# A decoder layer on one core: the order of TensorE's tiled fp32 steps, and of ScalarE's and VectorE's steps with them

## What is computed

```
h = x
z = rms_norm(h, norm_mix) @ w_in                          # 1024 x 3328
y_rwkv = rwkv7_time_mix(z[:, :1792], ...)                 # 8 heads x 64, a recurrence over tokens
y_moba = moba_attention(q, k, v from z[:, 1792:])         # 8 heads x 64, causal, one block of 256
h = h + concat(y_rwkv, y_moba) @ w_mix_out                # 1024 x 1024
h = h + cross_attention(rms_norm(h), rms_norm(mem))       # 4 heads x 256; w_xq, w_xkv, w_xo
a = square(relu(rms_norm(h, norm_ffn) @ w_ff1))           # 1024 x 4096
h = h + a @ w_ff2                                         # 4096 x 1024
out = rms_norm(h, norm_final)
```

## Time and profile before

| what | value |
|---|---|
| median of 3 runs | 471.38 us (470.81 to 471.77) |
| profiled execution, its own time | 470.57 us |
| its span, first to last instruction | 468.8 us |
| mean granted TensorE clock | 0.996 |
| PE busy | 453.8 us, 97% |
| DVE, ACT, POOL busy | 322.0, 236.6, 35.1 us |

### The profile page before, as it was taken

How to read it: one execution, slowest core, us unless ns; L and a number is a source line. 1 busy time by engine, 2 the same in 40 slices (tenths; PEclk the granted TensorE clock), 3 DMA queues, 4 the chain that set the end, 5 groups by cost and what they waited for, 6 DMA issues and landing times.

```text
span 468.8 us, 10481 instructions
## 1 busy us (share of the span) xinstructions
PE 453.8 (97%) x4470; PEld 410.1 (87%) x4470; DVE 322.0 (69%) x487; ACT 236.6 (50%) x373; POOL 35.1 (7%) x51
## 2 busy tenths in 40 slices
PE   4999999989999999999999999999999999999994
PEld 4999999989899879999998898888888888888883
DVE  4688999897485557668766368876555656574746
ACT  5789833252444426436444455545465545454534
POOL 8200000000000000071000001340000000000000
PEclk9999999999999999999999999999999999999998
DMA  7973534606050432462552165655546565756502
GB/s 246 334 226 119 180 95 142 215 5 184 3 194 15 153 119 89 137 225 89 180 181 89 35 189 189 218 181 179 180 147 213 185 197 166 251 185 218 188 2 89
DMA packets 60385, 73.05 MB, mean 156 GB/s; under 512 B 1314, under 2 KB 49524, under 8 KB 60340
## 3 DMA queue, kind: packets, MB, share of 16 engines
q1 hardware_dynamic: 60260, 72.14, 48.3%
q0 software_dynamic: 80, 0.26, 0.1%
HBM read 71.35 MB, written 1.05 MB: 154 GB/s over the span
## 4 chain that ended last, share of the span: by engine, by line
PE 90%; DVE 4%; DMA 1%; SPq 1%; ACT 1%; issue 1%; ACTq 0%; DVEq 0%
PE bank L534 13%; PE bank L549 11%; PE bank L550 10%; PE bank L551 10%; PE bank L566 6%; PE bank L568 6%; PE bank L567 6%; PE bank L536 6%; PE bank L915 2%; DMA raw<-in_w_in 1%; PE bank L502 1%; PE bank L503 1%; PE bank L504 1%; PE bank L939 1%; PE bank L488 1%
## 5 line engine op out<-in xcount | busy, mean ns | idle before, releaser
L1622 DVE TENSOR_TENSOR w_lo<-raw,w_hi 128x1024 fp32r<-128x1024 f32 x130 | 160.2, 1239 | 67.2 <-ACT w_hi L1114 67.1
L1114 ACT ACTIVATE w_hi<-raw 128x1024 fp32r<-128x1024 f32 x130 | 136.8, 1057 | 111.0 <-PE bank L551 51.8
L534 PE MATMUL bank<-op,w_hi 128*128 128x512 f32 x256 | 89.1, 398 | 0.0
L549 PE MATMUL bank<-op,w_hi 128*128 128x256 f32 x288 | 83.7, 291 | 0.2 <-DVE w_lo L1622 0.2
L550 PE MATMUL bank<-op,w_hi 128*128 128x256 f32 x288 | 81.4, 283 | 0.0
L551 PE MATMUL bank<-op,w_lo 128*128 128x256 f32 x288 | 81.4, 283 | 0.0
L536 PE MATMUL bank<-op,w_lo 128*128 128x256 f32 x224 | 62.8, 281 | 0.0
L549 PEld LDWEIGHTS bank<-op,w_hi 128*128 128x128 f32 x288 | 55.1, 191 | 1.3 <-issue 0.9
L550 PEld LDWEIGHTS bank<-op,w_hi 128*128 128x128 f32 x288 | 55.2, 192 | 0.2
L551 PEld LDWEIGHTS bank<-op,w_lo 128*128 128x128 f32 x288 | 55.1, 191 | 0.0
L534 PEld LDWEIGHTS bank<-op,w_hi 128*128 128x128 f32 x256 | 46.4, 188 | 8.9
(11 more groups left out here) (275 smaller groups left out, 712.6 us busy)
## 6 DMA issues: line engine op xcount, KB each, us to landing
raw<-in_w_ff SPq DMA_DIRECT2D x32, 1024.0 KB, 5.4
raw<-in_w_in SPq DMA_DIRECT2D x12, 1024.0 KB, 5.5
raw<-in_w_xkv SPq DMA_DIRECT2D x8, 1024.0 KB, 5.3
raw<-in_w_mix_out SPq DMA_DIRECT2D x4, 1024.0 KB, 5.0
raw<-in_w_xq SPq DMA_DIRECT2D x4, 1024.0 KB, 5.0
raw<-in_w_xo SPq DMA_DIRECT2D x4, 1024.0 KB, 5.7
xval<-in_x SPq DMA_DIRECT2D x2, 512.0 KB, 4.7
raw<-in_w_in SPq DMA_DIRECT2D x2, 512.0 KB, 5.7
```

Source lines behind the costliest of these rows:

```text
L534: last = mm(b[:, :], wh[:, k, :], op_both[0][:, :, k, :], start=first, stop=final)
L549: mm(dst, wh[:, k, :], op_hi[which][:, k, :], start=first, stop=False)
L1114: op(view(w_hi), r, ACT.Copy).then_inc(hi_done, 1)
L1622: tt(view(w_lo), r, view(w_hi).bitcast(f32), ALU.subtract).then_inc(lo_done, 1)
```

## The change

The lists of calls of PE, ACT and DVE are written in another order. No instruction is added or removed, no shape changes, and one wait is added, on DVE in `bonus`. On PE the tiled steps stand together more often: `mats` in one piece for three, `outq` in one for four, `psi` in one for two, `pair_scores` and `pair_values` beside other tiled steps. The number of unbroken stretches of fp32 steps between quarters goes from 49 to 40; those with a tiled step in them from 26 to 14. A change of the tile from one instruction to the next occurs 64 times before and 43 times after; of these, 29 and 17 go from the whole array to a tile, as many go back, and 6 and 9 go from one tile to another. 23 and 10 stretches end in a tiled step, 26 and 30 in one of the whole array. The core of the diff:

```diff
 # PE
+            load(0, 0)
             params(0)
-            load(0, 0)
...
-            dense(2)
+            dense(1)
             params(1)
-            dense(2)
+            dense(5)
             spread(0)
...
-            dense(2)
-            vtokens()
             bonus()
             dense(2)
+            vtokens()
+            dense(1)
             mats(0, 0)
             mats(0, 1)
-            dense(1)
             mats(0, 2)
             mats(0, 3)
-            dense(3)
             mats(1, 0)
...
+            dense(4)
             right(0)
             right(1)
-            load(1, 2)
-            dense(4)
-            load(1, 3)
+            dense(1)
             right(2)
-            right(3)
-            dense(1)
             join(0, 0)
             join(0, 1)
-            dense(2)
+            right(3)
             join(1, 0)
-            dense(3)
+            join(1, 1)
+            dense(4)
             pair_scores(0)
-            join(1, 1)
-            dense(1)
             solve(0)
...
+            pair_values(0)
             outq(0, 0)
-            pair_flip(0)
             outq(0, 1)
             outq(0, 2)
-            pair_values(0)
-            dense(1)
-            pair_scores(1)
-            dense(1)
             outq(0, 3)
...
+            outq(1, 3)
+            pair_scores(1)
+            dense(6)
+            phi(0)
+            phi(1)
+            pair_flip(1)
...
             turn(3)
-            dense(1)
             values(3)
-            dense(46)
+            dense(58)
             rms(3)
-            dense(9)
+            dense(29)
             residual(0)
+            dense(6)
             residual(1)
-            dense(34)
+            dense(12)
             residual(2)
+            dense(32)
             residual(3)
-            dense(53)
+            dense(6)
 # ACT
             hi(1)
-            stats(0)
             hi(2)
             hi(3)
+            stats(0)
             hi(4)
+            stats(1)
             hi(5)
             follow(0)
-            stats(1)
...
 # DVE
             def bonus():
                 dve.wait_ge(pe_bonus, 1)
+                dve.wait_ge(dve_shift, 7)
...
             square(1)
-            lo(72)
+            add(2, 1)
+            lo(73)
+            lo(74)
             hidden(1)
...
```

More of the change, by code:

```diff
@@ L1031, in _ @@
             dense(1)
-            pair_flip(2)
             state(1)
-            dense(1)
+            pair_scores(2)
             state(2)
-            pair_values(2)
             dense(1)
             state(3)
+            dense(4)
+            state(4)
+            pair_flip(2)
             dense(1)
-            state(4)
-            dense(1)
+            pair_values(2)
             state(5)
@@ L1391, in _ @@
             right(0)
+            load(1, 2)
             hi(24)
-            load(1, 2)
+            hi(25)
             right(1)
+            right(2)
+            join()
             load(1, 3)
-            right(2)
             right(3)
-            join()
-            hi(25)
             hi(26)
@@ L1406, in _ @@
             pair_flip(0)
+            hi(29)
             pair_values(0)
-            hi(29)
             hi(30)
+            outq(0)
+            hi(31)
             pair_scores(1)
-            hi(31)
-            pair_flip(1)
-            outq(0)
             outq(1)
@@ L1416, in _ @@
             hi(33)
+            pair_flip(1)
             pair_values(1)
-            pair_scores(2)
             hi(34)
@@ L1514, in _ @@
             part(4, 1)
+            follow(36)
             hi(82)
-            follow(37)
             part(5, 0)
             hi(83)
+            hi(84)
+            follow(37)
+            hi(85)
             part(5, 1)
-            hi(84)
+            hi(86)
             follow(38)
-            hi(85)
-            hi(86)
             hi(87)
+            part(6, 0)
             hi(88)
-            part(6, 0)
-            rms(3)
-            residual(0)
             hi(89)
@@ L1601, in _ @@
             hi(129)
+            residual(3)
             finish()
@@ L2051, in _ @@
             load(0, 3)
+            params(1)
             lo(1)
-            diagonal_of(0)
-            params(1)
             lo(2)
             lo(3)
+            copies(0)
+            diagonal_of(0)
             spread_copy(0)
+            take(0)
             lo(4)
-            take(0)
+            copies(1)
+            lo(5)
             follow(0)
-            lo(5)
+            lo(6)
             take(1)
-            lo(6)
-            copies(1)
-            lo(7)
             follow(1)
             take(2)
+            lo(7)
             lo(8)
+            sides()
             lo(9)
+            follow(2)
             diagonal_of(1)
-            follow(2)
             take(3)
             sums()
+            lo(10)
+            key_norm()
             follow(3)
+            key_root()
             spread_copy(1)
-            key_norm()
-            lo(10)
-            key_root()
             lo(11)
+            keys(0)
             take(4)
-            keys(0)
             keys(1)
@@ L2101, in _ @@
             lo(18)
-            sides()
+            follow(6)
+            lo(19)
             load(1, 0)
+            take(8)
+            load(1, 1)
             bonus()
-            lo(19)
             lo(20)
-            load(1, 1)
-            take(8)
-            bonus_bias()
             mats(0)
-            take(9)
+            mats(1)
             lo(21)
             lo(22)
+            take(9)
             lo(23)
-            mats(1)
             blocks()
@@ L2146, in _ @@
             phi(2)
-            pair_values(1)
-            pair_scores(2)
-            pair_weigh(2)
-            take(15)
             lo(33)
             lo(34)
+            take(15)
+            pair_values(1)
             state(1)
             state(2)
+            pair_scores(2)
+            bonus_bias()
+            state(3)
             take(16)
-            state(3)
+            pair_weigh(2)
             lo(35)
+            state(4)
             lo(36)
-            state(4)
             state(5)
+            pair_values(2)
+            lo(37)
             state(6)
-            lo(37)
+            pair_scores(3)
             states_out()
-            pair_values(2)
+            pair_weigh(3)
             lo(38)
-            pair_scores(3)
+            deviation()
             take(17)
-            pair_weigh(3)
-            deviation()
             lo(39)
-            take(18)
             normalize()
             lo(40)
+            take(18)
             lo(41)
@@ L2193, in _ @@
             operand("mix", 0)
+            operand("mix", 1)
             lo(50)
-            operand("mix", 1)
             operand("mix", 2)
+            lo(51)
             operand("mix", 3)
+            lo(52)
+            rms(2)
             take(24)
-            lo(51)
-            lo(52)
+            take(25)
             lo(53)
-            rms(2)
-            take(25)
+            scores(0)
             lo(54)
-            scores(0)
             weigh(0)
+            lo(55)
             take(26)
-            lo(55)
             lo(56)
+            scores(1)
+            weigh(1)
+            take(27)
+            values(0)
             lo(57)
-            scores(1)
-            take(27)
-            weigh(1)
+            scores(2)
             lo(58)
-            values(0)
-            scores(2)
+            lo(59)
             weigh(2)
-            lo(59)
             values(1)
```

297 lines of the change are left out of this document (144 added, 153 removed).

## The result

The change makes the kernel slower: 486.39 us as the median of 4 runs (485.89 to 487.57) against 471.40 (470.81 to 471.77), a ratio of 1.0323 with a 95% interval of 1.0311 to 1.0335. The prediction was 467.6. The profiled execution took 485.89 us with a span of 483.9, 15.1 us more than the one before.

The account below looks back on a forecast made before the run. PE's own instruction list was taken as the bound, plus its few waits. Borders and tails -3.34, waits -0.9 and -0.2, start +0.65 gave -3.8 us, from 471.38 to 467.6, range 465.5 to 469.8.

Parts of the forecast that it names:

- The sum over borders: On PE, fewer ways into and out of tiled stretches and fewer stretch ends would save 3.34 us.
- The prices: Cost of a tiled stretch on PE beyond its work: 0.09 us going in, 0.11 coming back, plus the tail.
- the tail: Time at the end of a tiled stretch that is no work: 0.14 us for `mats`, 0.19 for `outq`.
- the -3.8 of the sum: Whole kernel: borders -3.34, PE's waits -0.9 and -0.2, start +0.65, together -3.8 us.
- the part on PE's order: With the same matmuls on PE, only border and tail prices count; the new order saves 3.34 us.
- Rival E: Long tiled stretches lower PE's clock, 2 to 3 us lost in each of three; about 474.6 us, chance 0.04.
- `join`: PE's 1.1 us wait for `blocks` before `join` shrinks by 0.9, PE coming later and `blocks` beginning and ending as before.
- The start: `spread(0)`, two quarters later, costs its own time, coming back and 0.2 us waiting for `stats(0)`: together a 0.65 us loss.
- B: Border price goes, but new waits through ACT and DVE between joined tiled steps add 2.1 us: 469.7 us, chance 0.15.
- D: Feed-forward stage: `down` waits for the moved-back `hidden` in all eight groups; slower, 475.6 us, chance 0.05.

Follow-up runs that it names:

- the probes: Fourteen short stretches of fp32 products of constants, on tiles or the whole array, added near the end of the kernel before, three quarters between two; 492.47 us in one execution.

## Why the prediction was wrong

- **The sum over borders, -3.34.** The prices were right, by the probes to 0.01 us in and out and 0.04 in the tail (0.10, taken as 0.14 for `mats`; no probe has the shape of `outq`, taken as 0.19). The sum left out the changes between two tiles, 6 before and 9 now, which at 0.11 take back 0.3. What doesn't lie in or behind a stop became 3.5 us shorter, waits and start included, against the -3.8 of the sum. That is a remainder and no kernel shows it alone, but it says that the gain came and is in the result.
- **The step that failed** is the first sentence of the part on PE's order: "The matmuls are the same, so the work is the same, and only these prices count." It took PE's rate in a long stretch to be that of the earlier trace rows, which were measured on 64 and 128 matmuls. It had no term for the supply of the instructions themselves, which costs 13.0 us of stops and up to 5.8 of low clock. The sign was in the trace of before: its instruction packets already stood 3.7 to 4 us apart around the four `mats` and the two `join`, so that a stretch twice as long had to outrun them. I read no view of that queue.
- **Rival E** named a slow clock, at 474.6 and a chance of 0.04, and for the wrong cause. The stops lower the clock, not the small tiles, and it is the smaller part of the loss.
- **`join`.** PE's wait fell to 0.3 us as forecast, but `blocks` did not begin "when it did": it starts at 93.54 us, not 90.69. `mats` itself was done sooner (85.3 for 88.0), but `lo(23)` before `blocks` waits for ACT and that for PE's quarters, as the prediction says, and the stops of 1.8 and 1.2 us had made these late. PE came to `join` late by the same stops, so the distance between the two stayed as forecast.
- **The start.** `spread(0)` took 0.39 us at 20.23, with no wait for `stats(0)`: 0.2 us of the 0.65 did not come.
- **B and D.** Against B, the waits for ACT and DVE in the result are 0.3 us more at one place (1.0 for 0.7, at the end of cross-attention) and 0.8 less at `join`. Against D, `down` never waits for `hidden`: `hidden(1)` ended at 319.0 and PE came at 320.3.

## What to carry to other kernels

Before steps of short instructions are joined, count the instructions, not only the time: here a block of 256 (64 fp32 calls) came no faster than one in 3.3 to 4 us, PE could begin it 1.2 us after its packet had landed at the soonest, and what a border saved was 0.3 us while a long stop cost 2 to 5. A wait "issue" on an engine, at distances of whole blocks of all its instructions, is the sign of it, and quarters of long matmuls between short ones are what keeps it away. Under such a bound, and with ACT's and DVE's lists written to match, joining steps brought 0.4% and 0.15% in the two orders held to 300 instructions in a stretch; the one held to 400 lost 0.6%.

## What the runs showed that I had not expected

- The longest stops stand at 5.75, 14.75, 18.75, 41.75 and 42.75 blocks of 256, and last 1.8 to 3.9 us. A stretch of 256 instructions once stopped (2.5 us), and one of 512 once had no stop inside, but one of 1.6 us 16 instructions behind it.
- A stop of 2.4 us with no other work on PE let the clock fall to the 1.2 GHz level. PE went on at 467.53, and the clock was full again in the row from 471.30.
- A change between two tiles costs 0.11 to 0.12 us inside a stretch, as much as the way to the whole array.
- What sets the start of a packet stays open: two in three start when PE is at 0.6 to 0.9 of a block beyond the number of packets before them, most others later, some only when PE is dry.
